# Encoder step with differential and stick-breaking attention: which query block of a prompt step comes first

## What is computed

```
n = rms_norm(x);  q, k, v of both mixers = n @ w_in          (3072 columns)
differential attention, 4 heads, two 64-wide maps per head, 128-wide values:
    s = q k^T / 8 - slope * |distance|, block-causal in chunks of 64
    a = softmax(map 0) - lam * softmax(map 1);   o = a v, normalised per head
stick-breaking attention, 8 heads of 64, strictly causal:
    a = sigmoid(z) * prod of (1 - sigmoid(z)) over the later keys;   o = a v
h = x + [o_diff | o_sb] @ w_out
y = h + swiglu(rms_norm(h));  final rms_norm
```

## Time and profile before

| What | Value |
|---|---|
| Runs of the kernel before | 1680.92 us median of 3 (1680.82 to 1683.18) |
| The profiled execution's own time | 1682.26 us |
| Span of that profile (first to last instruction) | 1680.5 us |
| Mean granted TensorE clock | 0.971 |
| TensorE matmuls busy | 1566.6 us, 93% |
| VectorE busy | 669.2 us, 40% |
| ScalarE busy | 401.2 us, 24% |
| POOL busy | 365.0 us, 22% |
| `attend` | about 345 to 725 us of the span |

### The profile page before, as it was taken

The page is one execution under the profiler, slowest core; times in us unless marked ns, Lnnn a source line. Parts: engine busy times, 40 slices in busy tenths (PEclk is TensorE's granted clock), DMA queues, the critical chain, the costliest instruction groups (busy, mean ns, idle before and its releaser), DMA issues. The chain is left out here.

```text
span 1680.5 us, 22021 instructions
## 1 busy us (share of the span) xinstructions
PE 1566.6 (93%) x9072; PEld 1339.9 (80%) x9072; DVE 669.2 (40%) x1063; ACT 401.2 (24%) x887; POOL 365.0 (22%) x257
## 2 busy tenths in 40 slices
PE   6999999858888999959989999999999999999997
PEld 5778777646676766638869898999989899998986
DVE  4602220067775777936531313233231323223135
ACT  3201101136666766612211010100001010000102
POOL 2412220100000000431134142222413222241311
PEclk9999999979998999979989999999999999999999
DMA  6332111243333443461111120111112111120202
GB/s 225 128 114 97 47 41 48 76 130 91 104 99 102 139 130 108 132 196 51 48 54 47 38 76 30 46 38 38 44 32 76 38 38 38 38 63 14 63 0 107
DMA packets 165402, 127.07 MB, mean 76 GB/s; under 512 B 13568, under 2 KB 142968, under 8 KB 165304
## 3 DMA queue, kind: packets, MB, share of 16 engines
q1 hardware_dynamic: 157912, 112.31, 22.5%
q10 hardware_dynamic: 7392, 13.37, 2.2%
HBM read 103.23 MB, written 22.41 MB: 75 GB/s over the span
## 5 line engine op out<-in xcount | busy, mean ns | idle before, releaser
L1563 DVE TENSOR_TENSOR hidden<-ps_u,gate 128x364 f32<-128x364 f32 (+1 forms) x66 | 35.3, 535 | 444.6 <-ACT gate L1509 444.6
L1509 ACT ACTIVATE gate<-ps_g 128x364 f32<-128x364 f32 (+1 forms) x66 | 31.3, 474 | 678.5 <-PE ps_u L1599 678.5
L1541 DVE TENSOR_TENSOR h_all<-ps_y,h_all 128x512 f32<-128x512 f32 (+1 forms) x198 | 136.7, 690 | 131.6 <-PE ps_y L1617 131.6
L1597 PE MATMUL ps_g<-n2T_hi,shared 128*128 128x364 f32 (+1 forms) x528 | 174.4, 330 | 3.7 <-DVE shared L1553 3.7
L289 PE MATMUL ps_proj<-shared,nT_hi 128*128 128x512 f32 (+1 forms) x432 | 169.8, 393 | 6.1 <-DVE nT_lo L232 6.1
L1598 PE MATMUL ps_g<-n2T_lo,shared 128*128 128x364 f32 (+1 forms) x528 | 174.2, 330 | 0.0
L1599 PE MATMUL ps_g<-n2T_hi,shared 128*128 128x364 f32 (+1 forms) x528 | 174.2, 330 | 0.0
L1598 PE MATMUL ps_u<-n2T_lo,shared 128*128 128x364 f32 (+1 forms) x528 | 173.5, 329 | 0.0
L1597 PE MATMUL ps_u<-n2T_hi,shared 128*128 128x364 f32 (+1 forms) x528 | 173.5, 329 | 0.0
L1599 PE MATMUL ps_u<-n2T_hi,shared 128*128 128x364 f32 (+1 forms) x528 | 173.4, 329 | 0.0
L291 PE MATMUL ps_proj<-shared,nT_lo 128*128 128x512 f32 (+1 forms) x432 | 170.7, 395 | 0.0
(11 more groups left out here) (171 smaller groups left out, 2785.1 us busy)
## 6 DMA issues: line engine op xcount, KB each, us to landing
staging<-in_w_gate SPq DMA_DIRECT2D x22, 512.0 KB, 5.0
staging<-in_w_up SPq DMA_DIRECT2D x22, 512.0 KB, 6.3
staging<-in_w_down SPq DMA_DIRECT2D x22, 512.0 KB, 3.6
w_raw<-in_w_in SPq DMA_DIRECT2D x5, 2048.0 KB, 8.2
x_sb<-in_x_prompt SPq DMA_DIRECT2D x8, 512.0 KB, 4.1
staging<-in_cache_diff_k SPq DMA_DIRECT2D x16, 256.0 KB, 2.9
v<-in_cache_diff_v SPq DMA_DIRECT2D x16, 256.0 KB, 5.0
staging<-in_cache_sb_k SPq DMA_DIRECT2D x16, 256.0 KB, 3.1
```

The source lines that it names most:

```text
L1541: nc.vector.tensor_tensor(hh, ps_y[0:n, y % 4], hh, ALU.add).then_inc(y_added, 1)
L1597: nc.tensor.matmul(out, w_h, x_h, start=(k == 0), stop=False)
```

## The change

`parts(x)` lists block 7-p first and block p second, and the offsets in z follow. All that is derived from it follows too: of a prompt step the block with more keys is scored, exponentiated or kept, combined or scanned, turned, multiplied and stored first. The set of instructions and of DMAs is unchanged, and so are their sizes, but for which unit is where. The sample steps are untouched.

```diff
         if is_sample(x):
             return [(NB, 0, LIVE)]
-        return [(p, 0, P * (p + 1)), (NB - 1 - p, P * (p + 1), P * (NB - p))]
+        return [(NB - 1 - p, 0, P * (NB - p)), (p, P * (NB - p), P * (p + 1))]
```

## The result

The changed kernel takes 1640.49 us (median of 4 runs, 1638.98 to 1641.31) against 1680.87 us before. The ratio is 0.9756, with a 95% interval of 0.9739 to 0.9773. That is 40.4 us faster, where 33.3 were forecast. It lies at the very edge of the range of 1640 to 1668 (against the median of 1680.92 the ratio gives 1639.9, just outside it). The direction and the mechanism were right; the sum was a fifth too small, because two of its terms were: the clock, and what the turns' waits leave.

What follows compares the result with a forecast made beforehand. TensorE was taken as nearest to a bound, with its idle waits for VectorE's weights winnable: 20.0 - 1.2 - 0.4 + 6.8 + 1.1 + 7 = 33.3 us, from the median 1680.92 to 1647.6 us; range 1640 to 1668.

Steps and rivals of the forecast that it cites:

- The clock: Behind long waits in differential and stick-breaking heads, the lowered granted clock was to recover: 7 us won (0 to 10.8).
- The chain: Differential steps' first turn waits for a long combine behind position 3's piece; waits fall from 25.9, 20.0 us won.
- The start: Attention's early turn, idle 3.88 us, was to come 2.4 us earlier than 360.56, leaving 1.5 us of wait.
- Bank waits: Differential heads: later readings cost nothing (8.5 us at the other end); next head's first unit, three times 0.4: -1.2 us.
- the VectorE rival: Differential heads: VectorE sets the pace and later readings reach TensorE; only 18.3 us won, 1662.6 us; chance 0.14.
- The passage: Between the two kinds of heads, TensorE's 3.5 us wait for ScalarE grows by about 0.4 (0 to 1.3).
- Stick-breaking: Three of four scan waits go, 6.8 us; piece behind the long sample scan starts earlier, 1.1 us (0 to 1.4).
- The last head: VectorE is full and POOL's split ends the stage, so the order gives 0, with 0.8 us as upper end.
- The clock rival: Small waits left in the attention keep the clock down: 26.3 us won, 1654.6 us; chance 0.14.
- Nothing comes of it: In the attention, VectorE's and ScalarE's total work sets the pace; waits reappear at the next bank: 1681 us; chance 0.04.

Runs made afterwards that it cites:

- the fastest kernel: Changed kernel with the long distance table scaled an iteration later and ScalarE copying the turned group ahead of the sample's exponential: 1635.9 us.
- the last experiment: 12 identity turns put ahead of the attention's first turned group, against the fastest kernel: 1637.61 us.
- the one with the piece behind: Kernel before, old order, with the last exponential and last combine of differential iterations ahead of position 3's prepared piece: 1669.04 us.

## Why the prediction was right or wrong, point by point

The mechanism was right. The step of the prediction that failed most is its clock term: "I take two thirds, since not all the work scales: 7 us (0 to 10.8)". Filling the waits measured 11.2 us by the medians and 12.2 in the profiles, above even the bound, from which the range's end of 1640 was made. Next comes the term for the turns, 20.0 us where 23.6 were measured.

- *The clock*: 7 forecast, 11.2 to 12.2 measured, too small in two ways. Not all the work was to scale, but the four stretches at p = 1 cost 6.7 us of the 7.4 that the bound gave and the two others 3.0 of 3.4, nine tenths. And the first stretch, behind the wait of 3.88 us, was left out altogether; filling that wait saved 2.5.
- *The chain* (differential turns): right, and shown from three sides: by the trace after, by the kernel that turns the short part first, and by the one that shortens the chain in the old order. The size was low: 20.0 forecast, 23.6 measured (25.9 to 2.3). The step that failed is "I put the long combine where the short one stands in the trace". It left 0.6, 0.4 and 0.1 us at p = 1, 2 and 3, and in the trace after 0.37 (once) and 0.16 (three times) are left at p = 1, and nothing at p = 2 and 3. At p = 1 the combine stood 0.1 us behind the start of the prepared piece's turn (412.12 and 412.03) and now starts 0.4 us ahead of it, because the unit that VectorE reads ahead of it has 256 keys where it had 512.
- *The start*: 1.5 us of the first wait were to be left and 1.42 are, but the agreement is luck. The combine was to start at 356.83 and the turn to come 2.4 us earlier than 360.56. In the trace after VectorE and TensorE both reach this place 1.9 us later, and the turn comes only 0.55 us earlier:

```profile
357.94 0.66 PE L1007 MATMUL ps_z<-ident,staging 128*128 128x128 f32 x4
358.68 1.28 DVE L884 SCALAR_TENSOR_TENSOR z<-z,ratio 128x1024 f32<-128x1024 f32 x1
360.01 0.55 PE L1057 MATMUL ps_aT<-ident,z 128*128 128x128 f32 x3 [1.42 <-DVE z L884]
```

  Of the 1.9 us, 0.67 are an attention that began later in this execution (its first turn of a piece at 346.54 instead of 345.87). Besides, the bank wait of 1.03 us is new, and the clock came back at 352.3 us instead of 349.3; how these two share the rest is not shown.
- *Bank waits*: -1.2 forecast, 3 x (1.18 - 0.78) = 1.2 measured, and one of 0.35 us in step 0 besides. The 8.5 us of later readings did not reach TensorE, as forecast; the VectorE rival falls. VectorE is busy 31.65 of 36.64 us in a head now, so its play is small.
- *The passage*: -0.4 forecast, 3.5 to 3.7 measured.
- *Stick-breaking*: the three waits of 6.8 us are gone, and three of 0.18 for a copy are new. For the pieces 1.1 us were forecast and 1.05 measured, by luck: the forecast counted two waits of 0.70 us and had most of both gone, but there are three (the third is named `shared` in the view), and each fell to 0.35.
- *The last head*: 0 forecast, 0.1 measured, and shown by the run with the old order there.
- *The clock rival*, with the Trainium skill's rule on short idles between groups ("TensorE: Matmul & The Clock Gate", "A second HAM failure mode: psum-queue depth-cycling"): inside the heads of the trace after, waits of 0.16 to 1.18 us, with bank waits among them, left the granted clock at 1.00, so there the trace does not agree with it. At the start of the attention it can agree: in the kernel with the w_out pieces earlier, whose code is the changed kernel's up to there, the clock fell at 354.4 us, behind two waits of 0.58 and 0.72 us and after 3.4 us at 1.00, and stayed down for 10.2:

```profile
353.92 0.50 PE L1037 MATMUL ps_z<-shared 64*128 64x512 f32 x2 [0.72 <-DVE lowest L857]
...
354.40:364.60 10.20, 9.23 (x41) 5.74 (x38) 8.00 (x24) 5.00 (x13) 0.00 (x0) 0.50 0.17 51
```

- *Nothing comes of it* fell. The prediction had read "Perfetto Trace Analysis" (the Trainium skill, "Identifying the Most-Contended Engine"), which says to optimize the engine of the highest occupancy first, as if only less work on that engine could help. TensorE's work is the same, and its idle time was what was won, so the measurement speaks against that reading and not against the page.

Not named by any wait are 0.2 to 0.3 us in each of three steps per head: p = 2 without its old wait was 7.0 and is 6.8, p = 3 without its waits 6.7 and is 6.4, the sample 9.4 and is 9.2. Some 3 us in four heads; what they are stays open. The other way, the part behind the attention is 1.5 us longer in the profile after (from POOL's end at 724.42 and 681.73 to the end of the span), with the same code there. With these two the profiles' difference of 41.2 us closes: the first turn comes 0.5 us earlier, from there to the last head TensorE's named waits are 26.8 us fewer (36.9 to 10.1), the clock gives 12.2 and the unnamed part 3.0, the last head 0.1, and 1.5 are lost behind the attention.

## What to carry to other kernels

In a software pipeline with one queue per engine, look at which part of a step is finished last in its iteration and who needs it first: put the long part early in the queue, and let the part behind the unrelated work of the late positions be the one whose first reader comes late. A gain in TensorE's waits has to be counted with the clock that falls behind them, and filling the wait with harmless matmuls sizes that directly. In the last head, where VectorE is full nearly from end to end, the order inside its queue changed nothing, and POOL's work moved forward didn't shorten the stage, since VectorE has a share in that work. And where one wait is removed, look for the next one behind it: here three stood in a row.

## What the hardware showed that was not expected

Whether the clock falls behind a wait of 1.4 us differs between executions. The first turn of the attention waits 1.42 or 1.43 us in six of the profiles, of kernels with the same code up to there (their edits act later). The granted clock of the 5.9 us behind it was 1.00 once (the changed kernel), 0.71 twice (the differential steps alone; the fastest kernel) and 0.50 three times (the far table later; that with w_out earlier; the old order in the last head). The four numbers in the expectation of the last experiment were read from one fixed stretch (360.10 to 366.00) in every kernel; one of the four, that with w_out earlier alone (0.62), had waited 0.72 us and lost its clock before.

Inside the heads no wait of 1.37 us or less brought it down, and all eight of 3.35 us did (four each in the kernel before and in that with the stick-breaking steps alone). Between the two it is open. Behind 2.06 us before step 20 it stayed up in the kernel before (the step took 8.86 us), and fell in the one with the differential steps alone and in the one with the piece behind (10.39 and 10.43 us). In the kernel that turns the short part first it fell behind seven of the eight waits of 2.57 to 2.68 us and behind two of the four of 2.2 us, and stayed at 1.00 behind the others. The stretches behind two of its waits of 2.57 us, the first with the fall and the second without:

```profile
466.73:471.40 4.67, 4.67 (x28) 4.11 (x28) 1.45 (x7) 1.86 (x5) 0.00 (x0) 0.63 0.03 8
513.19:517.90 4.71, 4.71 (x41) 4.22 (x41) 2.43 (x10) 3.07 (x10) 0.00 (x0) 1.00 0.49 140
```

Even the 3.4 us at the passage left it at 1.00 once, in the fastest kernel. The changed kernel's rows for that wait and stretch, and those of the kernel with the table scaled later:

```profile
360.01 0.55 PE L1057 MATMUL ps_aT<-ident,z 128*128 128x128 f32 x3 [1.42 <-DVE z L884]
...
360.10:366.00 5.90, 5.34 (x41) 3.81 (x41) 5.76 (x20) 4.00 (x11) 0.00 (x0) 1.00 0.30 88
```

```profile
360.42 0.90 PE L1057 MATMUL ps_aT<-ident,z 128*128 128x128 f32 x3 [1.43 <-DVE z L884]
...
360.10:366.00 5.90, 5.58 (x25) 3.95 (x26) 4.53 (x15) 3.43 (x8) 0.00 (x0) 0.50 0.27 82
```

The same stretch holds 41 matmuls at the one clock and 25 at the other. The step took 6.16 and 7.84 us. So a wait of this length has no one price, and an expectation for a single run can be off by 1.7 us for it. The changed kernel's profile happened to be one in which nothing was lost there.
